# Three stage borders of a two-block transformer kernel: where TensorE claims its banks, and behind which products the turns of the fourth token tile stand

## The chip, the core and the metric

The kernel runs on one core of a Trainium2 chip. A core has TensorE (PE in the profile; PEld is its weight load), VectorE (DVE), ScalarE (ACT), GpSimd (POOL) and SyncE (SP), which run side by side, each through its own list of instructions in order, and wait for one another by semaphores. The metric is the device time of one execution in microseconds (us).

## The reference, cut to what matters

512 tokens of width 1024 go through two blocks. The first mixes attention and pooling by two gates, applies an output product `w_o`, a norm and a residual sum, and then a convolved, gated feed-forward part. The second starts with a norm and a wide product `w_in`, and goes on with two attentions, an output product, a mixture of 32 experts and a last gate.

```python
def first_block(x, ...):
    ...
    mix = (g_a * y_a + g_b * y_b) @ w_o[l]                       # border 1 stands ahead of this product
    x = x + rms_norm(mix, norm_mix_post[l])
    f = conv_gated_ffn(rms_norm(x, norm_ffn_pre[l]), w_up[l], ...)   # border 2: norm, then x @ w_up
    x = x + rms_norm(f, norm_ffn_post[l])
    return x

def second_block(x, ...):
    ...
    a = rms_norm_2(h, g_mix[i])                                  # border 3: norm, then a @ w_in
    proj = a @ w_in[i]
    ...
    h = h + hier_moe(rms_norm_2(h, g_ffn[i]), w_rg[i], w_re[i], w1[i], w3[i], w2[i])
    ...
```

Everything is float32.

## The kernel before, in words

**Tiles.** The tokens are four tiles of 128 (`t` = 0 to 3). X stays in on-chip memory as 128 partitions x 4 tiles x 1024. The eight PSUM banks take the results of TensorE, 128 x 512 each. Which product goes into which bank is fixed by a table (`ps`). `claim(e, key)` waits until the product that stood in that bank before has been read out (semaphore `out_of`, one for each bank), `filled` waits until the bank is written, and `taken` until it has been read.

**Products in three parts.** A dense weight is loaded in units of 128 x 2048. ACT rounds a unit to its high part `w_hi` (L607) and DVE takes the rest as `w_lo` (L612); the activations exist as `HTH` and `HTL` in the same way. A product is then three matmuls for each piece of 128 rows: high by high, high by low, low by high. `split_ready` waits for the low part of a unit (`split_lo_done`). The next unit's split waits until the unit in its buffer has been used; for some units the semaphore `w_used` tells that.

**A norm between two products.** For each token tile DVE scales X by the reciprocal root (L685, semaphore `n_scaled`), TensorE turns the scaled tile with 8 transposes (`norm_pe`, L717: "the turns" of a tile), ACT copies the turned halves to `HTH` (L671) and DVE writes `HTL` (L691). `ht_ready(e, R, t)` waits for that L691. Before the scaling stands the residual sum of the tile: L737 or L745 and L764/L770 (squares and products), L773, L780 (X), L665, L667, L680. The four tiles go through this staggered, in one list on ACT and one on DVE (`stagger`), and the split of a weight unit stands in the middle of it.

**Border 1, the output product (`wo_pe`, about 302 us).** The last products ahead of it are the gates (L788), whose results ACT takes by a sigmoid (L1218) and DVE multiplies (L1267). `wo_pe` claims four banks, one for each token tile, then runs the product of the first half of the rows for four tiles (`j` = 0, 12 matmuls a tile, L1245, from `MIXH` and `MIXL`), and the second half.

**Border 2, the start of the feed-forward part (`ffn_pe`, about 351 to 382 us).** In this order: the turns of tile 1, `uv` for tile 0, the turns of tile 2, `uv` for tile 1, the turns of tile 3, `ug` for tiles 0 and 1 (two outputs `j` of 24 matmuls with 256 columns), then `uv` and `ug` for tiles 2 and 3. All these are L800.

**Border 3, the start of the second block (`qk_pe`, about 720 to 748 us).** Turns of tile 1; the first half of unit pair `in2` for tiles 0 and 1 (L831); turns of tile 2; the second half for tiles 0 and 1 (L819); turns of tile 3; both halves for tiles 2 and 3. After the last first-half product TensorE raises `w_used`, for which ACT's next split (L607) waits, and behind that split stand ACT's squares of the results (L1572), DVE's sums and scalings (L1627, L1638, L1648) and POOL's rotations (L1657, L1659, semaphore `h_qn`). TensorE turns the rotated tiles (L1555) between the products of the next units.

The order on each engine is written out by hand in these functions; no scheduler moves it. The loads of the weights are issued by SP (L878, and L2209 for the experts), each as soon as its place in memory is free.

Of the kernel before, what the change touches and what calls it, by code (L numbers as in the profile page):

```python
# [17 lines left out]
TT, KD = 4, 8  # L18
# [112 lines left out]
def build(nc, x_d, wd, w1_d, w3_d, w2_d, cols_d, rows_d, cst_d, wr_d, wpg_d, pT_d, tb_d, nb_d, out_d):  # L131
    with ExitStack() as ctx:
# [3 lines left out]
        def sem(name):  # L136
            return ctx.enter_context(nc.semaphore(name))
# [83 lines left out]
        w_used, split_hi_done, split_lo_done = sem("w_used"), sem("split_hi_done"), sem("split_lo_done")  # L221
# [247 lines left out]
        def claim(e, key):  # L469

            b, _, emptied = ps.at[key]
            if emptied:
                e.wait_ge(out_of[b], emptied)
            return bank[b], full[b]
# [36 lines left out]
        for n in range(NDENSE):  # L511

            b = n if n < NS else (n - TWO) % 2 if n >= TWO else (2, 3, 1, 0)[(n - A_TWO) % 4] if n >= A_TWO else n % 2
# [108 lines left out]
        def split_ready(e, key):  # L622
            e.wait_ge(split_lo_done, split_index(unit[key]) + 1)
# [84 lines left out]
        def norm_pe(e, R, t):  # L708
            if R != 4:
                e.wait_ge(n_scaled, 4 * R + t + 1)  # L710
            for h in range(2):
                if R == 4:
                    e.wait_ge(n_gained, 2 * t + h + 1)
                b, fills = claim(e, ("n", R, t, h))
                for k in range(4):
                    at = (4 * h + k) * 128
                    m = e.transpose(b[:, k * 128:(k + 1) * 128], norm_xs(R, t)[:, at:at + 128], ident)  # L717
                m.then_inc(fills, 1)

        def ht_ready(e, R, t):  # L720

            for h in range(2):
                taken(e, ("n", R, t, h))
# [67 lines left out]

        ht = [[v[:, k, :] for k in range(KD)] for v in (HTH, HTL)]

        def gemm3_T_part(e, key, outs, ts, last):

            wh, wl = parts(key, KD)
            for j, (b, fills) in enumerate(outs):
                for k in range(KD):
                    for i, (w, src) in enumerate(((wh, HTH), (wh, HTL), (wl, HTH))):
                        m = e.matmul(b[:, ts], w[:, k, j * 128:(j + 1) * 128], src[:, k, ts],  # L800
                                     start=(k == 0 and i == 0), stop=(k == KD - 1 and i == 2))
                if last:
                    m.then_inc(fills, 1)
# [10 lines left out]
        def gemm_tok_part(e, key, j, t, out, low):  # L814

            w = list(parts(key, 4))[low]
            for k in range(4):
                for i, src in enumerate((HTH,) if low else (HTH, HTL)):
                    m = e.matmul(out[:, :], src[:, 4 * j + k, t * 128:(t + 1) * 128], w[:, k, :],  # L819
                                 start=(j == low == k == i == 0), stop=(j == 1 and low == 1 and k == 3))  # L820
            return m

        def high_ready(e, key):
            e.wait_ge(split_hi_done, split_index(unit[key]) + 1)

        def gemm3_tok(e, key, j, t, out):

            wh, wl = parts(key, 4)
            for k in range(4):
                for i, (src, w) in enumerate(((HTH, wh), (HTH, wl), (HTL, wh))):  # L830
                    m = e.matmul(out[:, :], src[:, 4 * j + k, t * 128:(t + 1) * 128], w[:, k, :],  # L831
                                 start=(j == k == i == 0), stop=(j == 1 and k == 3 and i == 2))
            return m
# [405 lines left out]
        def mix_tok(e, key, j, t, out):  # L1239

            wh, wl = parts(key, 4)
            for k in range(4):
                hi, lo = mix_parts(4 * j + k)
                for i, (src, w) in enumerate(((hi, wh), (hi, wl), (lo, wh))):
                    m = e.matmul(out[:, :], src[:, t * 128:(t + 1) * 128], w[:, k, :], start=(j == k == i == 0),  # L1245
                                 stop=(j == 1 and k == 3 and i == 2))
            return m
# [44 lines left out]


        def wo_pe(e):
            bs = [claim(e, ("wo", t, 0)) for t in range(TT)]
            for j in range(2):
                split_ready(e, ("wo", j))
                e.wait_ge(mt_lo, 4 * j + 4)
                for t in range(TT):
                    m = mix_tok(e, ("wo", j), j, t, bs[t][0])  # L1300
                    if j:
                        m.then_inc(bs[t][1], 1)
                if j == 0:
                    m.then_inc(w_used, 1)
            for t in range(TT):
                b, fills = claim(e, ("wo", t, 1))
                for j in range(2):
                    split_ready(e, ("wo", 2 + j))
                    m = mix_tok(e, ("wo", 2 + j), j, t, b)
                m.then_inc(fills, 1)  # L1310
                if t == 2:
                    norm_pe(e, 1, 0)
# [33 lines left out]
        def ffn_pe(e):  # L1346
            outs = {v: [claim(e, (v, j)) for j in range(2)] for v in ("uv", "ug")}
            norm_pe(e, 1, 1)
            split_ready(e, ("uv", 0))
            ht_ready(e, 1, 0)  # L1350
            gemm3_T_part(e, ("uv", 0), outs["uv"], slice(0, 128), False)
            norm_pe(e, 1, 2)
            ht_ready(e, 1, 1)
            gemm3_T_part(e, ("uv", 0), outs["uv"], slice(128, 256), False)
            norm_pe(e, 1, 3)
            split_ready(e, ("ug", 0))
            gemm3_T_part(e, ("ug", 0), outs["ug"], slice(0, 256), False)
            ht_ready(e, 1, 2)
            ht_ready(e, 1, 3)
            gemm3_T_part(e, ("uv", 0), outs["uv"], slice(256, 512), True)  # L1360
            gemm3_T_part(e, ("ug", 0), outs["ug"], slice(256, 512), True)
            for s, (us, ds) in enumerate(FFN):
                for u in us:
                    for j in range(2):
                        for name in ("uv", "ug"):
                            if u:
                                split_ready(e, (name, u))
                                gemm3_T(e, (name, u), 128 * j, *claim(e, (name, 2 * u + j)), *ht)
                for t in range(TT):
                    for h in range(2):  # L1370
                        b, fills = claim(e, ("dn", s, t, h))
                        down_part(e, s, t, h, b).then_inc(fills, 1)
                    if s == LAST and t == 2:
                        norm_pe(e, 2, 0)
# [136 lines left out]
        def qk_pe(e):  # L1511
            bs = [claim(e, ("h", 0, t)) for t in range(TT)]
            norm_pe(e, 2, 1)
            for t0 in (0, 2):
                for j in range(2):
                    if (t0, j) == (0, 1):
                        high_ready(e, ("in2", 1))
                        for t in (0, 1):
                            gemm_tok_part(e, ("in2", 1), 1, t, bs[t][0], 0)
                        split_ready(e, ("in2", 1))  # L1520
                        for t in (0, 1):
                            gemm_tok_part(e, ("in2", 1), 1, t, bs[t][0], 1).then_inc(bs[t][1], 1)
                        norm_pe(e, 2, 3)
                        continue
                    split_ready(e, ("in2", j))
                    for t in (t0, t0 + 1):
                        ht_ready(e, 2, t)
                        m = gemm3_tok(e, ("in2", j), j, t, bs[t][0])
                        if j:
                            m.then_inc(bs[t][1], 1)  # L1530
                        elif t == 3:
                            m.then_inc(w_used, 1)
                    if t0 == 0:
                        norm_pe(e, 2, 2 + j)
            for G in (1, None):
                u = 2 if G else 4
                bs = []
                for j in range(2):
                    split_ready(e, ("in2", u + j))
                    for t in range(TT):  # L1540
                        if j == 0:
                            bs.append(claim(e, ("h", 1, t) if G else ("hv", t)))
                        m = gemm3_tok(e, ("in2", u + j), j, t, bs[t][0])
                        if j:
                            m.then_inc(bs[t][1], 1)
                            qk_turn_pe(e, 4 * (G is None) + t)
                        elif t == 3:
                            m.then_inc(w_used, 1)
# [1655 lines left out]
```

## Time and profile before

| | us |
|---|---|
| median of 3 runs | 1600.0 (1598.81 to 1601.59) |
| the profiled execution | 1599.1 |
| its span, first to last instruction | 1597.2 |
| TensorE busy | 1535.8 (96%) |
| DVE / ACT / POOL busy | 718.2 / 531.1 / 164.6 |
| mean granted clock of TensorE | 0.993 |

The profile is of one execution. A row of the timeline begins with the start and the duration; what stands in brackets at its end is how long the engine was idle before it and who ended that. Matmuls overlap: at full clock one of 512 columns starts about 0.23 us after the one before while its row says 0.39 us, so the distance of starts is what counts.

### The profile page before, as it was taken

The page shows a single profiled execution, that of the slowest core. Times are in us where ns is not written, and L with a number is a line of the kernel's source. Part 1 is how long each engine was busy: PE and PEld are TensorE (multiplying, and loading weights), DVE is VectorE, ACT ScalarE, POOL GpSimd, SP SyncE. Part 2 cuts the span into 40 slices and gives each one's busy share as a digit, 9 for nine tenths or more (in the row PEclk, how much of TensorE's full clock was granted, in tenths as well). Part 3 has the DMA queues.
Part 4 walks back from the last instruction along what each step waited for, and adds up shares of the span by engine and source line. Part 5 has one row for each costly group of instructions (what it writes and reads, how often), then busy time and mean ns, then how long its engine had stood idle before and what let it go on. Part 6 is the DMA issues. An engine that isn't in the chain of part 4 may idle for free.

```text
span 1597.2 us, 19641 instructions
## 1 busy us (share of the span) xinstructions
PE 1535.8 (96%) x7802; PEld 1079.7 (68%) x7802; DVE 718.2 (45%) x1208; ACT 531.1 (33%) x910; POOL 164.6 (10%) x172
## 2 busy tenths in 40 slices
PE   6899999999999999999999999999999999999898
PEld 5666688788888888887777777754444444444367
DVE  5335423455544444468565788432132132132164
ACT  5334422344333423344454577331011011010042
POOL 1013110002211111111300210011000000000000
PEclk9999999999999999999999999999999999999999
DMA  7111322213221323222110231779999999999951
GB/s 271 52 54 60 146 104 105 92 54 119 106 105 57 119 89 106 105 92 81 52 54 27 70 143 56 305 277 387 421 421 421 421 421 420 418 421 421 421 244 54
DMA packets 45437, 311.22 MB, mean 195 GB/s; under 512 B 5136, under 2 KB 5648, under 8 KB 10016
## 3 DMA queue, kind: packets, MB, share of 16 engines
q1 hardware_dynamic: 42336, 296.22, 46.6%
q0 software_dynamic: 3008, 13.72, 2.4%
q8 instruction: 64, 1.05, 0.3%
q14 instruction: 29, 0.24, 0.0%
HBM read 301.52 MB, written 8.39 MB: 194 GB/s over the span
## 4 chain that ended last, share of the span: by engine, by line
PE 87%; DVE 4%; DMA 3%; ACT 3%; issue 2%; DVEq 0%; ACTq 0%; POOLq 0%
PE bank L788 21%; PE bank L2460 13%; PE bank L831 8%; PE bank L1385 6%; PE bank L2476 6%; PE bank L840 6%; PE bank L2443 4%; PE bank L2493 4%; PE bank L1245 3%; PE bank L2659 3%; DMA M<-in_w 3%; PE bank L857 1%; PE bank L800 1%; PE bank L848 1%; PE bank L1986 1%
## 5 line engine op out<-in xcount | busy, mean ns | idle before, releaser
L612 DVE TENSOR_TENSOR w_lo<-M,w_hi 128x2048 fp32r<-128x2048 f32 x73 | 168.8, 2317 | 186.0 <-ACT w_hi L607 186.0
L2460 PE MATMUL bank<-M 128*64 128x512 f32 x1024 | 227.4, 595 | 4.3 <-DMA M<-in_w 4.3
L607 ACT ACTIVATE w_hi<-M 128x2048 fp32r<-128x2048 f32 x73 | 139.0, 1911 | 157.7 <-PE bank L788 56.9
L788 PE MATMUL bank<-HTH,w_hi 128*128 128x512 f32 x432 | 168.1, 389 | 0.0
L788 PE MATMUL bank<-HTL,w_hi 128*128 128x512 f32 x432 | 168.1, 389 | 0.0
L788 PE MATMUL bank<-HTH,w_lo 128*128 128x512 f32 x432 | 168.0, 389 | 0.0
L2460 PEld LDWEIGHTS bank<-M 128*64 128x64 f32 x1024 | 71.5, 137 | 139.8 <-issue 138.6
L2476 PE MATMUL bank<-M 128*64 128x512 f32 x512 | 113.8, 595 | 1.8 <-DMA M<-in_w 1.8
L2618 DVE TENSOR_TENSOR X<-bank,X 128x512 f32<-128x512 f32 x69 | 46.6, 689 | 112.9 <-PE bank L2493 112.8
L788 PEld LDWEIGHTS bank<-HTH,w_lo 128*128 128x128 f32 x432 | 81.1, 188 | 16.9
L788 PEld LDWEIGHTS bank<-HTH,w_hi 128*128 128x128 f32 x432 | 81.1, 188 | 16.8
L788 PEld LDWEIGHTS bank<-HTL,w_hi 128*128 128x128 f32 x432 | 81.1, 188 | 16.7
L2476 PEld LDWEIGHTS bank<-M 128*64 128x64 f32 x512 | 35.9, 137 | 71.6 <-issue 71.5
L2565 ACT ACTIVATE YH<-bank,st 128x512 fp32r<-128x512 f32 x32 | 22.0, 688 | 184.7 <-PE bank L2476 183.3
L831 PE MATMUL bank<-w_hi,HTH 128*128 128x512 f32 x184 | 75.2, 409 | 0.3 <-DVE HTL L691 0.3
L831 PE MATMUL bank<-w_hi,HTL 128*128 128x512 f32 x184 | 72.7, 395 | 0.0
L831 PE MATMUL bank<-w_lo,HTH 128*128 128x512 f32 x184 | 72.4, 393 | 0.0
L2608 DVE SCALAR_TENSOR_TENSOR YL<-bank,st,YH 128x512 fp32r<-128x512 f32 x32 | 24.0, 751 | 104.4 <-ACT YH L2565 103.9
L2595 DVE TENSOR_TENSOR M<-M,bank 128x512 f32<-128x512 f32 x16 | 11.0, 688 | 133.1 <-PE bank L2460 120.4
L1385 PE MATMUL bank<-w_hi,AH 128*128 128x512 f32 x176 | 68.6, 389 | 0.0
L1385 PE MATMUL bank<-w_hi,AL 128*128 128x512 f32 x176 | 68.5, 389 | 0.0
L1385 PE MATMUL bank<-w_lo,AH 128*128 128x512 f32 x176 | 68.5, 389 | 0.0
(365 smaller groups left out, 2875.6 us busy)
## 6 DMA issues: line engine op xcount, KB each, us to landing
M<-in_w SPq DMA_DIRECT2D x192, 1024.0 KB, 10.1
M<-in_wd SPq DMA_DIRECT2D x78, 1024.0 KB, 4.8
M<-in_nb SPq DMA_DIRECT2D x4, 1536.0 KB, 6.5
X<-in_x SPq DMA_DIRECT2D x4, 512.0 KB, 9.2
M<-in_rows POOLq DMA_DIRECT2D x4, 512.0 KB, 6.1
M<-in_tb POOLq DMA_DIRECT2D x8, 256.0 KB, 4.0
rowb<-in_rows POOLq DMA_DIRECT2D x4, 512.0 KB, 5.6
xs_parts<-XSH POOLq DMA_DIRECT2D x1, 2048.0 KB, 10.6
```

The costliest lines, as they stand in the source:

```text
L607: e.activation(hi[:, :], slots[slot_of[n]], ACT.Copy).then_inc(split_hi_done, 1)
L612: e.tensor_tensor(lo[:, :], slots[slot_of[n]], hi[:, :], ALU.subtract).then_inc(split_lo_done, 1)
L788: m = e.matmul(out[:, :], w[:, k0 + k, n0:n0 + 128], v[k], start=(k == 0 and i == 0), stop=(k == len(hi) - 1 and i == 2))
L831: m = e.matmul(out[:, :], src[:, 4 * j + k, t * 128:(t + 1) * 128], w[:, k, :], start=(j == k == i == 0), stop=(j == 1 and k == 3 and i == 2))
L840: m = e.matmul(out[:, :], w[:, k, n0:n0 + 128], src[:, k, :], start=(k == i == 0), stop=(k == 7 and i == 2))
L1245: m = e.matmul(out[:, :], src[:, t * 128:(t + 1) * 128], w[:, k, :], start=(j == k == i == 0), stop=(j == 1 and k == 3 and i == 2))
L1385: m = e.matmul(out[:, :], src[:, a, t * 128:(t + 1) * 128], w[:, i % 2, h * 512:(h + 1) * 512], start=(i == 0 and q == 0), stop=(i == len( ...
L2443: m = e.matmul(b[:, kk * 256:(kk + 1) * 256], v[:, t, k * 128:(k + 1) * 128], S[:, t, :], start=(t == 0 and q == 0), stop=(t == 3 and q == 1))
L2460: m = e.matmul(b[64 * s:64 * s + 64, :], Xe[:, 4 * kh + k, o + C * s:o + C * s + C], unit_w(key, 4)[:, k, :], start=(kh == 0 and k == 0), ...
L2476: m = e.matmul(b[64 * s:64 * s + 64, :], hT[p % 2][:, kk * 128 + 64 * s:kk * 128 + 64 * s + 64], unit_w(key, 2)[:, k, h * 512:(h + 1) * 51 ...
L2493: m = e.matmul(b[:, :], ST[p % 6][:, t * 128:(t + 1) * 128], Y[p % 3][:, h * 512:(h + 1) * 512], start=(p == SCAT[i][0] and q == 0 and not ...
L2659: m = e.matmul(out, x[:, k, t * 128:(t + 1) * 128], w[:, k % 4, cs], start=start and k == ks[0], stop=stop and k == ks[-1])
```

## The change: one wait cut into four, and turns moved behind other products

In `wo_pe` the claim of a tile's bank moves from the head of the function to the head of that tile's product in the first pass. In `ffn_pe` the turns of tile 3 move behind the first of the two `ug` outputs for tiles 0 and 1, and the wait for the `ug` unit moves ahead with it; `gemm3_T_part` gets an argument for which outputs it runs. In `qk_pe` the loop is written out: the first half for tile 2 stands ahead of the turns of tile 3, and then tile 2 is finished before tile 3 begins, where before both had their first half ahead of their second. No instruction is added or taken away on any engine, and ACT, DVE, POOL and SP keep their order.

```diff
-        def gemm3_T_part(e, key, outs, ts, last):
+        def gemm3_T_part(e, key, outs, ts, last, js=range(2)):
...
-            for j, (b, fills) in enumerate(outs):
+            for j in js:
+                b, fills = outs[j]
...
         def wo_pe(e):
-            bs = [claim(e, ("wo", t, 0)) for t in range(TT)]
+            bs = []
             for j in range(2):
                 split_ready(e, ("wo", j))
                 e.wait_ge(mt_lo, 4 * j + 4)
                 for t in range(TT):
+                    if j == 0:
+                        bs.append(claim(e, ("wo", t, 0)))
                     m = mix_tok(e, ("wo", j), j, t, bs[t][0])
...
             gemm3_T_part(e, ("uv", 0), outs["uv"], slice(128, 256), False)
+            split_ready(e, ("ug", 0))
+            gemm3_T_part(e, ("ug", 0), outs["ug"], slice(0, 256), False, [0])
             norm_pe(e, 1, 3)
-            split_ready(e, ("ug", 0))
-            gemm3_T_part(e, ("ug", 0), outs["ug"], slice(0, 256), False)
+            gemm3_T_part(e, ("ug", 0), outs["ug"], slice(0, 256), False, [1])
             ht_ready(e, 1, 2)
             ht_ready(e, 1, 3)
...
         def qk_pe(e):
             bs = [claim(e, ("h", 0, t)) for t in range(TT)]
             norm_pe(e, 2, 1)
-            for t0 in (0, 2):
-                for j in range(2):
...
+            split_ready(e, ("in2", 0))
+            for t in (0, 1):
+                ht_ready(e, 2, t)
+                gemm3_tok(e, ("in2", 0), 0, t, bs[t][0])
+            norm_pe(e, 2, 2)
+            high_ready(e, ("in2", 1))
+            for t in (0, 1):
+                gemm_tok_part(e, ("in2", 1), 1, t, bs[t][0], 0)
+            split_ready(e, ("in2", 1))
+            for t in (0, 1):
+                gemm_tok_part(e, ("in2", 1), 1, t, bs[t][0], 1).then_inc(bs[t][1], 1)
+            ht_ready(e, 2, 2)
+            gemm3_tok(e, ("in2", 0), 0, 2, bs[2][0])
+            norm_pe(e, 2, 3)
+            gemm3_tok(e, ("in2", 1), 1, 2, bs[2][0]).then_inc(bs[2][1], 1)
+            ht_ready(e, 2, 3)
+            gemm3_tok(e, ("in2", 0), 0, 3, bs[3][0]).then_inc(w_used, 1)
+            gemm3_tok(e, ("in2", 1), 1, 3, bs[3][0]).then_inc(bs[3][1], 1)
```

The order of TensorE's instructions at border 1 before, where the last gate product ends and the output product begins (`out_of3` is bank 3 being read out; `mt_lo` the low parts of the mixed rows):

```order
L788 MATMUL bank7<-HTL,w_hi1 128x512
L788 MATMUL bank7<-HTH,w_lo1 128x512
L1245 MATMUL bank0<-w_hi2,MIXH 128x512 [waits out_of3,split_lo_done,out_of2,mt_lo,out_of1,out_of0]
L1245 MATMUL bank0<-w_lo2,MIXH 128x512
L1245 MATMUL bank0<-w_hi2,MIXL 128x512
```

And of the changed kernel, with the first matmul of each token tile:

```order
L788 MATMUL bank7<-HTH,w_lo1 128x512
L1246 MATMUL bank0<-w_hi2,MIXH 128x512 [waits out_of0,mt_lo,split_lo_done]
...
L1246 MATMUL bank1<-w_hi2,MIXH 128x512 [waits out_of1]
...
L1246 MATMUL bank2<-w_hi2,MIXH 128x512 [waits out_of2]
...
L1246 MATMUL bank3<-w_hi2,MIXH 128x512 [waits out_of3]
```

The wait for bank 3 has moved from the first matmul to the 37th, behind three tiles of 12.

TensorE at border 3 before, from the low-part matmuls of tiles 0 and 1 (banks 6 and 7) on; tile 2 is bank 0, tile 3 bank 1, the turns go to banks 4 and 5, `w_hi0` is the first unit of the pair and `w_hi1` the second:

```order
L819 MATMUL bank7<-w_lo1,HTH 128x512 x4
L717 MATMUL bank4<-cst,M 128x128 [waits out_of4,n_scaled]
L717 MATMUL bank4<-cst,M 128x128 x3
L717 MATMUL bank5<-cst,M 128x128 [waits out_of5]
L717 MATMUL bank5<-cst,M 128x128 x3
L831 MATMUL bank0<-w_hi0,HTH 128x512 [waits out_of3,out_of2,split_lo_done]
...
L831 MATMUL bank1<-w_hi0,HTH 128x512 [waits out_of5,out_of4]
...
L831 MATMUL bank0<-w_hi1,HTH 128x512 [waits out_of3,out_of2,split_lo_done]
...
L831 MATMUL bank1<-w_hi1,HTH 128x512 [waits out_of5,out_of4]
```

And in the changed kernel:

```order
L820 MATMUL bank7<-w_lo1,HTH 128x512 x4
L832 MATMUL bank0<-w_hi0,HTH 128x512 [waits out_of3,out_of2]
...
L717 MATMUL bank4<-cst,M 128x128 [waits out_of4,n_scaled]
L717 MATMUL bank4<-cst,M 128x128 x3
L717 MATMUL bank5<-cst,M 128x128 [waits out_of5]
L717 MATMUL bank5<-cst,M 128x128 x3
L832 MATMUL bank0<-w_hi1,HTH 128x512
...
L832 MATMUL bank1<-w_hi0,HTH 128x512 [waits out_of5,out_of4]
...
L832 MATMUL bank1<-w_hi1,HTH 128x512
```

Twelve matmuls now stand between the products of tiles 0 and 1 and the turns of tile 3, and twelve between these turns and the first matmul that needs what they lead to. Border 2 moves in the same way, with 24 matmuls of 256 columns ahead of the turns and 24 behind.

## Rows read from the trace of the kernel before

**Rows 1.** The page's chain that ended last, by engine, as shares of the span.
```profile
PE 87%; DVE 4%; DMA 3%; ACT 3%; issue 2%; DVEq 0%; ACTq 0%; POOLq 0%
```

**Rows 2.** Waits of TensorE: who waited for whom, us in total, times, longest.
```profile
PE bank L2460 <- DMA M<-in_w: 4.3, 5, 1.3
PE bank L2476 <- DMA M<-in_w: 1.8, 3, 1.3
```

**Rows 3.** Timeline of TensorE at border 1: start, duration, instruction.
```profile
301.84 0.39 PE L788 MATMUL bank<-HTH,w_lo 128*128 128x512 f32 x1
304.11 0.47 PE L1245 MATMUL bank<-w_hi,MIXH 128*128 128x512 f32 x1 [1.88 <-DVE M L1267]
...
309.45 0.39 PE L1245 MATMUL bank<-w_lo,MIXH 128*128 128x512 f32 x1
```

**Rows 4.** Timeline of DVE at border 1.
```profile
296.12 2.49 DVE L1275 TENSOR_TENSOR MIXL<-M,MIXH 128x512 fp32r<-128x512 f32 x4
...
303.06 0.69 DVE L1267 TENSOR_TENSOR M<-bank,M 128x512 f32<-128x512 f32 x1 [3.84 <-ACT M L1218]
303.66 3.58 DVE L1278 TENSOR_TENSOR HTL<-M,HTH 128x512 fp32r<-128x512 f32 x4
```

**Rows 5.** Stretches: length, busy us of each engine, granted clock, DMA share, GB/s.
```profile
305.00:308.20 3.20, 3.20 (x10) 2.47 (x9) 2.45 (x4) 2.43 (x2) 1.06 (x2) 0.52 0.00 0
734.00:737.00 3.00, 1.17 (x10) 1.12 (x10) 1.45 (x2) 0.67 (x2) 0.00 (x0) 1.00 0.47 199
751.00:766.00 15.00, 15.00 (x72) 12.40 (x71) 13.69 (x17) 6.38 (x8) 10.69 (x8) 1.00 0.27 89
864.80:868.00 3.20, 3.20 (x9) 2.53 (x8) 1.90 (x5) 1.31 (x4) 0.00 (x0) 0.52 0.01 5
1300.00:1400.00 100.00, 100.00 (x508) 47.39 (x506) 21.83 (x34) 10.11 (x16) 2.33 (x4) 1.00 1.01 420
```

**Rows 6.** The chain that ended last, in time: pieces of 192 products.
```profile
382.32 43.55 PE bank L788 x192
```

**Rows 7.** Timeline of TensorE at border 2.
```profile
362.54 0.28 PE L800 MATMUL bank<-HTH,w_lo 128*128 128x128 f32 x1
363.95 1.09 PE L717 MATMUL bank<-cst,M 128*128 128x128 f32 x8 [1.14 <-DVE M L685]
364.80 0.37 PE L800 MATMUL bank<-HTH,w_hi 128*128 128x256 f32 x1
...
366.92 0.28 PE L800 MATMUL bank<-HTH,w_lo 128*128 128x256 f32 x1
```

**Rows 8.** Timeline of DVE at border 2.
```profile
356.99 2.29 DVE L612 TENSOR_TENSOR w_lo<-M,w_hi 128x2048 fp32r<-128x2048 f32 x1 [0.83 <-ACT w_hi L607]
...
365.28 1.29 DVE L691 TENSOR_TENSOR HTL<-bank,HTH 128x512 fp32r<-128x512 f32 x2 [1.38 <-ACT HTH L671]
```

**Rows 9.** Timeline of TensorE at border 3.
```profile
732.06 1.97 PE L819 MATMUL bank<-w_lo,HTH 128*128 128x512 f32 x8
735.87 1.09 PE L717 MATMUL bank<-cst,M 128*128 128x128 f32 x8 [1.83 <-DVE M L685]
```

**Rows 10.** Timeline of DVE at border 3.
```profile
732.63 1.28 DVE L691 TENSOR_TENSOR HTL<-bank,HTH 128x512 fp32r<-128x512 f32 x2
...
737.19 1.29 DVE L691 TENSOR_TENSOR HTL<-bank,HTH 128x512 fp32r<-128x512 f32 x2 [1.38 <-ACT HTH L671]
```

**Rows 11.** Behind border 3: ACT's split, POOL's rotations, TensorE's turns of tile 3.
```profile
742.47 1.92 ACT L607 ACTIVATE w_hi<-M 128x2048 fp32r<-128x2048 f32 x1 [3.02 <-PE bank L831]
761.48 2.79 POOL L1657 TENSOR_TENSOR M<-M 128x256 f32<-128x256 f32 x1
764.34 0.73 POOL L1659 TENSOR_TENSOR M<-M 128x256 f32<-128x256 f32 x1
770.94 0.60 PE L1555 MATMUL bank<-cst,M 128*128 128x128 f32 x4
```

**Rows 12.** Waits of SP's queue for the expert weights.
```profile
SPq L2209 <- PE bank L2460: 294.8, 63, 34.3
```

More of the change, by code:

```diff
@@ L1513, in qk_pe @@
             norm_pe(e, 2, 1)
-            for t0 in (0, 2):
-                for j in range(2):
[L1516 to L1534, printed above, removed]
+            split_ready(e, ("in2", 0))
[16 more added lines that the diff above has]
+            gemm3_tok(e, ("in2", 1), 1, 3, bs[3][0]).then_inc(bs[3][1], 1)
             for G in (1, None):
```

## The prediction

> **What bounds the kernel now.** I read the chain that ended last first, then TensorE's waits, then the timelines around the three places that the change touches, and last the far end of the program. The chain is TensorE's for 87% of the span [rows 1]: what takes an idle stretch out of TensorE's list, and puts none in, shortens the kernel, unless something behind it runs on a clock of its own. In the timeline each border shows one such stretch. At border 1 the last gate matmul starts at 301.84 and the first of the output product at 304.11, after 1.88 us idle that a read-out by DVE ended [rows 3]. At border 2 the turns of tile 3 start at 363.95, with 1.14 us idle before them until DVE's scaling of that tile was done [rows 7]. At border 3 the same turns start at 735.87 after 1.83 us idle [rows 9]. The idle figures count from the modelled end of a matmul, so I work with starts: 192 products in a row took 43.55 us, 0.227 us each, with a claim of a bank at every 24th [rows 6].
>
> **Border 1.** With no wait the output product would start at 301.84 + 0.23 = 302.07; it started at 304.11: 2.04 us. What was waited for is bank 3 alone: DVE's last L1267 runs from 303.06 to 303.75, and it had been idle for 3.84 us, so all that it did before had ended by 299.2, the low parts of the first four mixed rows among it (296.12 + 2.49 = 298.6) [rows 4]. In the new order bank 3 is asked for at the 37th matmul, 302.07 + 36 x 0.227 = 310.2, 6.5 us after it is free. The second half of the rows starts 48 matmuls in, at 313.0; the low parts that it needs end at 303.66 + 3.58 = 307.2 [rows 4]. So nothing takes the place of the wait, and 2.04 us go. The three claims that now stand between tiles cost nothing, as the claims inside the 192 products don't.
>
> There is a second part. From 304.11 to 309.45 stand 16 starts, 5.34 us where 16 x 0.227 = 3.63 are due, and the stretch from 305.0 to 308.2 shows a granted clock of 0.52, that is the lower level, 1.2 GHz, where stretches of steady work show 1.00 [rows 3, 5]. Before it fell, TensorE had stood still for 2 us; at border 3, after nearly as long a stop, the clock stayed at 1.00 [rows 5, 9]. So the stop makes the fall possible but doesn't always bring it. With the stop gone 5.34 - 3.63 = 1.71 us go too, where an execution had them. I take half, 0.85; the ends are 0 and 1.71.
>
> The Trainium skill (TensorE: Matmul & The Clock Gate, Part 1: The HAM clock gate) says that how many matmuls run slow differs between runs of one kernel. By that the 1.71 us are in some executions of the kernel before and not in others, and the sum would be 5.1 or 6.9 us and seldom between; the trace, which is one execution, cannot tell how often.
>
> **Border 2.** TensorE could have gone on at 362.54 + 0.11 = 362.65, the distance of starts of the 128-column matmuls there; the turns started at 363.95: 1.30 us. Now 24 matmuls with 256 columns come first. 17 of them took from 364.80 to 366.92, 0.125 each with the slower first [rows 7], so 24 take 3.0 us and the turns are reached at 365.6, 1.7 us after the tile is scaled. Their weight, the `ug` unit, is split by 356.99 + 2.29 = 359.3 [rows 8]; their inputs, tiles 0 and 1, are those that the `uv` products have just read. What could be late next is the low part of tile 3. DVE's L691 ended at 365.28 + 1.29 = 366.57, 2.62 us after the turns began [rows 7, 8]; so now it ends 2.6 + 0.1 us behind their start, and TensorE needs it after the turns (363.95 to 364.80, 0.85) and 24 matmuls (3.0), 3.85 us behind it. 1.1 us to spare. 1.30 us go, and all of it moves with border 1, since this chain of DVE and ACT starts from TensorE's own products.
>
> **Border 3.** The eighth low-part matmul ends its turn at 732.06 + 8 x 0.227 = 733.87; the turns started at 735.87: 2.00 us. In the new order tile 2's first half comes first. It needs L691 of tile 2, which ends at 732.63 + 1.28 = 733.91 [rows 9, 10]; with 0.15 us for the signal a new wait of 0.19 us stands there. Then 12 x 0.227 = 2.7 us of matmuls reach the turns at 736.8, 0.9 us after the scaled tile is there (735.87). L691 of tile 3 ended at 738.48, 2.61 us behind the turns [rows 10]; now TensorE wants it 0.84 + 2.7 = 3.6 us behind them: 0.8 us to spare. 2.00 - 0.19 = 1.81 us go.
>
> One thing here gets later. The release of `w_used` comes with tile 3's first half, formerly the 24th matmul behind the turns and now the 36th of a stretch that begins at 734.06 and has the turns in it: 734.06 + 36 x 0.227 + 0.84 = 743.1 plus its drain and two slower starts, 743.4, where ACT's split began at 742.47 [rows 11]. That is 1.0 us later, and queued behind this split are ACT's squares, DVE's sums and POOL's rotations of the first group. TensorE meets this chain again at the turns of rotated tile 3, at 770.94; POOL was done at 765.07 [rows 11]. Of these 5.9 us the change takes 1.0 + 1.8, and 3.1 are left. The unit that this split makes is wanted only after 48 more matmuls, at about 756.7. I price it at nothing.
>
> **The sum.** 2.04 + 0.85 + 1.30 + 1.81 = 6.0 us; without the clock 5.15, with all of it 6.86. Against the profiled execution, 1599.1: 1593.1 (1592.2 to 1594.0). The median of the runs shown is 0.9 above that execution, which may be chance among three; I go half the way and predict **1593.6 us**, 0.4% below the median. A measurement of this kernel can tell a difference from no change above about 0.2%, 3.2 us.
>
> **Does it reach the end?** In the expert stage the DMA moves 420 GB/s with TensorE busy all the time [rows 5], and TensorE waits for weights only for 4.3 + 1.8 us in sum [rows 2]. If that stream ran from a fixed start, time won before it would turn into waits for it. But SP's own queue waited 294.8 us for TensorE to give memory free [rows 12]: the stream starts, and fills, at TensorE's pace, and moves forward with it.
>
> **The rivals.**
> 1. *The gain is given back in the expert stage* (no change). A DMA engine share of 1.01 [rows 5] speaks for it: there the transfers are as full as TensorE. Against it is that the loads wait for TensorE. If it happened, the end would stay at the profiled 1599 to 1600. Chance 0.06.
> 2. *The clock falls elsewhere instead.* Five stretches of 0.52 stand in this trace, one of them at 864.8 [rows 5], inside attention, where TensorE stops often and briefly. Everything behind border 1 moves by 4 to 6 us, so which of these stops brings a fall is drawn again. Each is worth 1.7 us by the 16 starts of [rows 3]. Two more than before, and a gain of 5.15 is 1.75: 1600.0 - 1.75 = 1598.3. Chance 0.08.
> 3. *The later release at border 3 ends slower.* Place: POOL's rotations ahead of 770.94. Two instructions of one form took 0.73 and 2.79 us there [rows 11], and the eight for the first group 10.7 us in sum [rows 5]; if the new timing made all eight like the long one, 22.3. Above 3.1 us of delay TensorE stands: 11.6 - 3.1 = 8.5 us, and 1600.0 - 5.15 + 8.5 = 1603.4. Against it: nothing in the change gives POOL more work, and the mean of the eight, 1.3 us, is far from the long one. Chance 0.03.
> 4. *One of the three borders keeps its stop*, say because tile 3's low part is late and uses up the 0.8 or 1.1 us: the gain is then 3.3 to 4.9 us, 1595.3 to 1597. Chance 0.10.
>
> **How the numbers follow.** The forecast itself, all three stops gone, has 0.73; its own range is 1591.3 to 1596. To hold 8 in 10 I take in rival 4 and a part of rival 2, and a little below for executions in which a fall in attention goes too: 1591.0 to 1597.6. Faster by over 0.2% (below 1596.8) are the forecast and most of rival 4: 0.84. Within 0.2%: rivals 1 and 2 and the rest of rival 4, 0.13. Slower: rival 3, 0.03.
>
> **What the changed profile would show.** TensorE's waits: no row from L1267 to the output product, and no idle ahead of the turns at borders 2 and 3; at border 3 instead about 0.2 us until L691. Border 1: starts at 0.227 us from the first matmul on, granted clock 1.00. Border 2: turns of tile 3 some 3 us behind the `uv` products. The first split of ACT behind border 3 later against TensorE's stretch, and no wait of TensorE at the turns of the rotated tiles. Behind 750, the same distances as before, all 5 to 7 us earlier, to the end. The prediction is wrong if a wait for L691 of over 1 us appears at border 2 or 3, or if TensorE's waits for the expert weights grow by what the borders gave.

## The result and the profile after

| | before | changed |
|---|---|---|
| median, 6 runs each | 1599.4 us (1597.43 to 1601.59) | 1592.46 us (1586.69 to 1593.08) |
| profiled execution / its span | 1599.1 / 1597.2 | 1593.08 / 1591.2 |
| TensorE busy | 1535.8 | 1536.0 |

The ratio is 0.9951, 95% interval 0.9935 to 0.9966: 0.49% faster, and the forecast of 1593.6 lies 1.1 us above the median. On another chip (e5 below), with 12 runs of the changed kernel beside 35 of the one before, the ratio was 0.9966 (0.9952 to 0.9981), 1592.45 against 1598.23 us. TensorE does as much as before; it stands still less.

TensorE's waits in the changed kernel (who waited for whom, us in total, times, longest):

```profile
PE bank L717 <- DVE M L685: 9.9, 2, 9.4
...
PE bank L2461 <- DMA M<-in_w: 2.9, 4, 1.4
PE bank L2477 <- DMA M<-in_w: 2.8, 3, 1.3
...
PE bank L832 <- DVE HTL L691: 0.3, 1, 0.3
```

No row from L1267 to the output product is left. The scaled tile is waited for at the program's start and once more, no longer at borders 2 and 3. The waits for expert weights are 5.7 us in sum where they were 6.1 [rows 2]: nothing was given back there.

Border 1, TensorE's timeline:

```profile
302.46 0.39 PE L788 MATMUL bank<-HTH,w_lo 128*128 128x512 f32 x1
302.69 0.39 PE L1246 MATMUL bank<-w_hi,MIXH 128*128 128x512 f32 x1
...
306.32 0.39 PE L1246 MATMUL bank<-w_lo,MIXH 128*128 128x512 f32 x1
```

From the last gate matmul to the first of the output product 0.23 us, and 3.86 us to its 17th, where [rows 3] have 2.27 and 7.61. Borders 2 and 3:

```profile
362.42 1.03 PE L717 MATMUL bank<-cst,M 128*128 128x128 f32 x8
363.22 0.36 PE L801 MATMUL bank<-HTH,w_hi 128*128 128x256 f32 x1
...
720.26 0.47 PE L832 MATMUL bank<-w_hi,HTH 128*128 128x512 f32 x1 [0.33 <-DVE HTL L691]
...
728.75 0.84 PE L820 MATMUL bank<-w_lo,HTH 128*128 128x512 f32 x3
729.58 0.47 PE L832 MATMUL bank<-w_hi,HTH 128*128 128x512 f32 x1
...
732.42 1.03 PE L717 MATMUL bank<-cst,M 128*128 128x128 f32 x8
733.21 0.48 PE L832 MATMUL bank<-w_hi,HTH 128*128 128x512 f32 x1
```

The turns of tile 3 have no idle in front of them at 362.42 and 732.42, as [rows 7, 9] had. The new wait of border 3 is the distance from the third of the matmuls at 728.75 (its start 729.20) to 729.58, 0.38 instead of 0.23: 0.15 us. It is the step that the prediction put in for the signal: DVE's L691 of tile 2 ends at 729.43, and the product that needs it starts at 729.58. The bracket at 720.26 belongs to tile 1 and was there before. DVE at the two borders:

```profile
363.69 1.29 DVE L691 TENSOR_TENSOR HTL<-bank,HTH 128x512 fp32r<-128x512 f32 x2 [2.94 <-ACT HTH L671]
...
733.69 1.29 DVE L691 TENSOR_TENSOR HTL<-bank,HTH 128x512 fp32r<-128x512 f32 x2 [2.36 <-ACT HTH L671]
```

At both it ends 2.56 us behind the start of the turns, where [rows 8, 10] have 2.62 and 2.61. Behind border 3, ACT's split, POOL's last rotation of the first group and TensorE's turns of that tile:

```profile
738.95 1.92 ACT L607 ACTIVATE w_hi<-M 128x2048 fp32r<-128x2048 f32 x1 [3.00 <-PE bank L832]
...
760.83 0.74 POOL L1660 TENSOR_TENSOR M<-M 128x256 f32<-128x256 f32 x1
...
764.70 0.60 PE L1556 MATMUL bank<-cst,M 128*128 128x128 f32 x4
```

Against the turns of tile 1 at border 3 the split begins 738.95 - 716.11 = 22.84 us behind them; before it was 742.47 - 720.59 = 21.88: the 1.0 us of the prediction. POOL is done 764.70 - 761.57 = 3.1 us ahead of need, where it was 5.9 [rows 11].

Four stretches of the changed kernel (columns as in [rows 5]):

```profile
80.00:83.30 3.30, 3.30 (x9) 2.53 (x9) 0.03 (x1) 0.00 (x0) 0.00 (x0) 0.50 0.25 97
302.50:306.50 4.00, 4.00 (x19) 3.34 (x18) 2.82 (x3) 2.60 (x5) 1.60 (x1) 1.00 0.00 0
729.00:733.00 4.00, 4.00 (x21) 3.06 (x20) 1.88 (x3) 0.71 (x3) 0.00 (x0) 1.00 0.48 203
1300.00:1400.00 100.00, 100.00 (x507) 47.40 (x506) 22.58 (x36) 11.48 (x18) 2.32 (x4) 1.00 1.01 420
```

Behind border 1 the clock stays at 2.4 GHz. Near 80 us, in attention, it is at 1.2 GHz in both executions.

### The profile page after: what moved, and what is told of

The parts are those of the page before. It is cut to its first block, busy times and chain, and to the rows that moved or that the text cites. A ratio compares the mean times of both kernels' runs of the same rounds, so it can differ in the third digit from the quotient of the medians.

```text
span 1591.2 us, 19637 instructions
## 1 busy us (share of the span) xinstructions
PE 1536.0 (97%) x7802; PEld 1080.1 (68%) x7802; DVE 718.0 (45%) x1208; ACT 531.0 (33%) x910; POOL 164.3 (10%) x172
## 4 chain that ended last, share of the span: by engine, by line
PE 89%; DVE 3%; DMA 3%; ACT 2%; issue 2%; DVEq 0%; ACTq 0%; POOLq 0%
PE bank L788 21%; PE bank L2461 13%; PE bank L832 8%; PE bank L1389 6%; PE bank L2477 6%; PE bank L841 6%; PE bank L2494 4%; PE bank L2444 4%; PE bank L2660 3%; PE bank L1246 3%; DMA M<-in_w 3%; PE bank L801 2%; PE bank L858 1%; PE bank L849 1%; PE bank L1987 1%
## 5 line engine op out<-in xcount | busy, mean ns | idle before, releaser
L788 PE MATMUL bank<-HTH,w_hi 128*128 128x512 f32 x432 | 168.1, 389 | 0.0
L788 PE MATMUL bank<-HTL,w_hi 128*128 128x512 f32 x432 | 168.1, 389 | 0.0
L788 PE MATMUL bank<-HTH,w_lo 128*128 128x512 f32 x432 | 168.1, 389 | 0.0
L788 PEld LDWEIGHTS bank<-HTH,w_hi 128*128 128x128 f32 x432 | 81.1, 188 | 16.9
L788 PEld LDWEIGHTS bank<-HTH,w_lo 128*128 128x128 f32 x432 | 81.1, 188 | 16.8
L788 PEld LDWEIGHTS bank<-HTL,w_hi 128*128 128x128 f32 x432 | 81.1, 188 | 16.8
## 6 DMA issues: line engine op xcount, KB each, us to landing
M<-in_nb SPq DMA_DIRECT2D x4, 1536.0 KB, 6.5
```

The source lines that it names most:

```text
L788: m = e.matmul(out[:, :], w[:, k0 + k, n0:n0 + 128], v[k], start=(k == 0 and i == 0), stop=(k == len(hi) - 1 and i == 2))
```

## Marks, for what single runs cannot tell

The time of one kernel varies over 9 us on a chip (before: 1593.15 to 1602.59 in 35 runs), more than any one border is worth. So each execution is read by distances between fixed instructions of TensorE. **A**: last gate matmul to the turns of tile 1 at border 2. **B**: from there to the first product of the next unit (L788). **C**: turns of tile 1 at border 3 to the first turns of a rotated tile (L1555). The kernel before and the changed one were profiled once each for the result, the others stand under The experiments.

| execution | changed borders | A | B | C |
|---|---|---|---|---|
| before | none | 48.42 | 31.90 | 40.73 |
| changed | 1, 2, 3 | 44.66 | 30.56 | 38.97 |
| e5 | 1, 2, 3 | 44.65 | 30.56 | 38.92 |
| e1 | 1 | 44.66 | 33.33 | 40.72 |
| e10 | 1, again | 44.65 | 33.38 | 40.71 |
| e2 | 2 | 48.41 | 30.59 | 40.71 |
| e3 | 3 | 48.43 | 31.90 | 38.97 |
| e4 | 2, 3 | 48.47 | 30.58 | 38.96 |
| e11 | 1, 3 | 44.66 | 31.90 | 38.93 |
| e6 | all, turns of border 3 late | 44.65 | 30.57 | 40.83 |
| e7 | all, turns of border 2 late | 44.66 | 32.48 | 38.95 |
| e8 | all, long stop at border 1 | 52.15 | 30.57 | 38.90 |
| e9 | all, short stop at border 1 | 45.77 | 30.58 | 38.96 |

A is 3.76 us shorter with the change, B 1.34, C 1.76: 6.86 us. The distance from B's end to the first turns of border 3 is 331.87 or 331.88 us in all thirteen. From C's end to the first turns of the last norm it is 780.60 before and 780.69 changed; over all thirteen it lies between 778.6 and 782.2 (e6 and e8), with the kernels with more and fewer changed borders mixed in it. What the borders gave is not taken back there; the profiled execution of the changed kernel shows 6.0 of it in its span, because it was 0.62 us later at border 1 (302.46 against 301.84) and lost 0.2 behind the last norm.

## The experiments

**e1, e2, e3, e4: one border at a time, and two without the first.** Each is the kernel before with the functions of those borders taken from the changed one, for e1:

```diff
-            bs = [claim(e, ("wo", t, 0)) for t in range(TT)]
+            bs = []
...
+                    if j == 0:
+                        bs.append(claim(e, ("wo", t, 0)))
```

> The kernel before with the change at border 1 alone (banks of the output product claimed tile by tile). Theory (each border's stop is worth its own idle, and the sum goes through to the end): from the last gate matmul to the first matmul of the output product 0.23 us instead of 2.27, no slow clock behind it; the turns of tile 1 of the next norm 3.75 us earlier against the last gate matmul; 2.0 to 3.8 us less in time. Rival 1 (the chain of DVE and ACT behind the output product keeps its own time): the turns of tile 3 at border 2 wait longer by what was won, and the gain shrinks below 1 us. Rival 2 (given back in the expert stage): the waits for expert weights grow by 2 us or more and the time stays within 0.5 us.

Measured: A 3.76 us shorter, C as before, but B 33.33 where it was 31.90. The time: 1595.84 against 1597.85 us, ratio 0.9988 (0.9974 to 1.0002), which does not tell it from no change. The waits at the turns of tile 3 of border 2 had not grown (1.14 us, as before), so rival 1 does not explain B. The clock does:

```profile
352.00:356.00 4.00, 4.00 (x38) 4.00 (x38) 3.50 (x6) 1.45 (x3) 0.53 (x1) 1.00 0.51 156
357.00:360.20 3.20, 2.75 (x13) 2.76 (x14) 1.20 (x3) 1.34 (x3) 0.00 (x0) 0.52 0.44 172
361.00:365.00 4.00, 4.00 (x36) 4.00 (x35) 2.29 (x1) 0.85 (x1) 0.00 (x0) 1.00 0.00 0
```

It fell at border 2 during the stop of 1.14 us (1.30 us by starts): the granted clock is 1.00 from 356.2 to 357.1 and 0.50 from 357.2 on, and the turns start at 357.44. 1.4 us of the 3.76 went back there. None of the theories in the expectation had that.

> The kernel before with the change at border 2 alone (turns of tile 3 behind the first ug output). Theory: no idle before the turns, no wait for the low part of tile 3, 1.30 us less from the uv products of tile 1 to the end of the border; time 1.3 us less, hardly above what can be measured. Border 1 still has its stop of 2.04 us, and whether the clock falls behind it is seen once more. Rival: the low part of tile 3 comes late, a wait for L691 of 0.5 us or more, gain under 0.8 us.

Measured: B 1.31 us shorter, no wait for L691; A unchanged, with the clock at 0.50 behind the stop. Ratio 0.9998 (0.9987 to 1.0008): too small to be seen in the time. The rival falls by the mark.

> The kernel before with the change at border 3 alone (tile 2's first half ahead of the turns of tile 3, tile 2 finished before tile 3). Theory: 1.8 us less between the low-part matmuls and the end of the stretch, and the same at every later mark; POOL's rotations about 1 us later than before, TensorE not waiting for them. Rival: TensorE waits at the turns of the rotated tiles, or for L691 of tile 3, and the gain is under 1 us.

Measured: C 1.76 us shorter. The distance from C's end to the last norm, 778.6 us, lies in the scatter given above. POOL is done 3.1 us ahead of TensorE's turns of the last rotated tile, as in the changed kernel, and there is no wait. Ratio 0.9980 (0.9967 to 0.9993), 1593.99 us. The rival falls.

> Borders 2 and 3 changed, border 1 left as before. Theory: 3.1 us less than before by the marks, 2.0 to 3.8 us more than with all three; the sum of the two alone within 0.3 us by the marks. Rival (they share one gain): less than the sum by over 1 us. The stop of border 1 stands here too: one more execution in which it is seen whether the clock falls behind it. If it falls in every one of the four executions with the stop, the clock part is 1.7 us and not half of that.

Measured: 1.32 + 1.77 = 3.09 us by the marks, the sum of the two alone (1.31 + 1.76) within 0.02; ratio 0.9985 (0.9971 to 0.9999), 1595.58 us. The first matmul of the output product in e2, in the timeline, and the stretch behind it, in the view of windows:

```profile
304.09 0.47 PE L1246 MATMUL bank<-w_hi,MIXH 128*128 128x512 f32 x1 [1.88 <-DVE M L1268]
```

```profile
305.10:308.30 3.20, 3.20 (x9) 2.53 (x8) 2.46 (x4) 2.43 (x2) 0.94 (x2) 0.50 0.00 0
```

The same two in e3:

```profile
301.26 0.47 PE L1245 MATMUL bank<-w_hi,MIXH 128*128 128x512 f32 x1 [1.88 <-DVE M L1267]
```

```profile
302.40:305.60 3.20, 3.20 (x10) 2.49 (x9) 2.46 (x4) 2.43 (x2) 0.82 (x2) 0.52 0.00 0
```

And in e4:

```profile
306.89 0.47 PE L1246 MATMUL bank<-w_hi,MIXH 128*128 128x512 f32 x1 [1.91 <-DVE M L1268]
```

```profile
308.20:311.40 3.20, 3.20 (x9) 2.52 (x8) 2.46 (x4) 2.43 (x2) 0.61 (x2) 0.50 0.00 0
```

With the kernel before that is four of four executions in which the clock fell behind this stop, though they reached it at times 6 us apart. In all four it fell when five or six matmuls had started at full clock, and eight distances of about 0.43 us followed where 0.23 are due: 1.6 us. The other 0.1 us of the 1.71 are slower starts at full clock. So the term of border 1 is 1.7 us in these executions, not half of it. Four executions cannot say that the clock always falls here: at a chance of one half each, four in a row come up once in sixteen times.

**e5: the changed kernel again**, no edit.

> The changed kernel once more, on the chip on which the single borders were tried, to have its marks twice. Theory: gate matmul to 17th matmul of the output product 3.85 us, as in the first execution, turns of tile 1 to the up products of border 2 30.6 us, border 3 39.0 us from the turns of tile 1 to the first turns of the rotated tiles; 6 to 7 us less than before. Rival (the first timing was lucky in the clock): 3 to 4 us less, with the same marks.

It ran on another chip than e1 to e4. Measured: the marks within 0.05 us of the first execution, and 1592.45 against 1598.23 us, 5.8 us less. The interval, 0.9952 to 0.9981, is 3.0 to 7.7 us less and so doesn't exclude the rival's 3 to 4 us by itself; the marks do. Four of the granted clocks among these runs say where most of the spread comes from:

| mean granted clock | before: runs, mean us | changed: runs, mean us |
|---|---|---|
| 0.990 | 6, 1601.2 | none |
| 0.993 | 3, 1599.7 | 4, 1593.4 |
| 0.996 | 9, 1597.1 | 1, 1589.2 |
| 0.998 or 0.999 | 6, 1593.9 | 3, 1588.0 |

At one clock the two kernels are 6 to 8 us apart, and each kernel varies by 5 to 7 us with the clock. Over the 35 runs of the kernel before, time and mean granted clock have a correlation of -0.89.

**e6 and e7: the turns still later.** In the changed kernel the turns of tile 3 go behind both products that now stand around them, at border 3

```diff
-            norm_pe(e, 2, 3)
             gemm3_tok(e, ("in2", 1), 1, 2, bs[2][0]).then_inc(bs[2][1], 1)
+            norm_pe(e, 2, 3)
```

> The changed kernel with the turns of tile 3 at border 3 behind both halves of tile 2 (24 matmuls ahead, none behind). Theory (the low part of tile 3 is ready 2.76 us behind the start of its turns, and 12 matmuls behind them cover that): TensorE waits 1.9 us for L691 in front of tile 3's first product, border 3 takes 40.9 us instead of 39.0, and all of the gain of border 3 is lost. Rival (what counts is only that the turns have no wait in front): no loss.

and at border 2 (`norm_pe(e, 1, 3)` behind the second `ug` output).

> The changed kernel with the turns of tile 3 at border 2 behind both ug outputs. Theory: TensorE waits 1.9 us for L691 behind the turns; from the turns of tile 1 to the products of the next unit 32.5 us instead of 30.6, or 34 if the clock falls behind this stop, where before, with its stop of 1.14 us ahead of the turns, it was 31.9. Rival: as in the run for border 3, no loss.

Measured, the first matmul behind the turns, at border 3 in e6 and at border 2 in e7:

```profile
734.75 0.47 PE L832 MATMUL bank<-w_hi,HTH 128*128 128x512 f32 x1 [1.66 <-DVE HTL L691]
```

```profile
364.88 0.36 PE L801 MATMUL bank<-HTH,w_hi 128*128 128x256 f32 x1 [1.66 <-DVE HTL L691]
```

C is 40.83, B 32.48. The stop has moved from in front of the turns to behind them, 1.9 us by starts, as the theory had it: the whole gain of border 3 is gone, and border 2 is 0.6 us worse than before. The rivals fall. The clock stayed at 1.00 in both (from 732 to 740 us in e6, from 362 to 370 in e7). What makes the change work is that products stand on both sides of the turns. In time neither could be told from the changed kernel: 1593.28 and 1592.83 us, ratios 0.9970 (0.9955 to 0.9984) and 0.9969 (0.9953 to 0.9984) to the one before.

**e8 and e9: other stops at border 1.** At the head of the changed `wo_pe` stands one more wait, in e8 `e.wait_ge(mt_lo, 8)`:

> The changed kernel with one more wait at the head of the output product, for the low parts of all eight mixed rows (which its second half needs anyway). Theory (the slow clock is a consequence of the stop, and costs 1.7 us whatever the stop's length): first matmul of the output product 5.5 us behind the last gate matmul, the 17th 10.9 us behind it, as against 3.85 without the stop and 7.6 with the one of before; 7 us more than the changed kernel. Rival (the slow clock costs in proportion to the stop): the 17th over 12 us behind. Rival (the clock falls at this place whatever stands there, by chance of this program's timing): also a slow stretch in the other run that has no stop.

in e9 `taken(e, ("g", 3, 1, 1))`:

> The changed kernel with one more wait at the head of the output product, for ACT's sigmoid of the last gate product: a stop of about 1 us, half of that of before (first matmul of the output product 1.3 us behind the last gate matmul). If the clock falls behind any stop at this place, the 17th matmul comes 6.6 us behind the gate matmul (1.3 + 3.6 + 1.7); if only behind a longer one, 4.9 us behind, as the stop of 1.14 us at border 2 did not bring the clock down in the kernel before.

Measured in e8, the first matmul of the output product and the stretch behind it:

```profile
307.50 0.79 PE L1246 MATMUL bank<-w_hi,MIXH 128*128 128x512 f32 x1 [5.05 <-DVE HTL L1279]
```

```profile
307.50:311.80 4.30, 4.30 (x10) 3.43 (x11) 2.29 (x1) 0.66 (x1) 0.57 (x1) 0.50 0.43 137
```

The first matmul came 5.44 us behind the gate matmul, the 17th 11.32, A is 7.49 us longer than in the changed kernel: 5.21 us of stop and 2.28 of slow clock. The slow part grew from 1.71 to 2.28 while the stop grew from 2.04 to 5.21, so neither theory is exact: it isn't a fixed price, and far from proportional. What it follows is how many matmuls start at the lower level. The granted clock was 0.50 already from 305.3 to 307.4 us, while TensorE stood still, so the product began slow: ten slow distances of starts, where the kernel before had eight. Measured in e9, the same two:

```profile
303.70 0.50 PE L1246 MATMUL bank<-w_hi,MIXH 128*128 128x512 f32 x1 [0.78 <-ACT M L1219]
```

```profile
303.00:310.00 7.00, 6.30 (x28) 5.18 (x29) 5.50 (x6) 4.65 (x6) 2.17 (x2) 1.00 0.06 11
```

The stop is 0.94 us by starts, the clock stayed up, and A is 1.11 us longer; the other 0.17 us are slower first starts at full clock. So the clock fell in five of five executions that stood still for 2.04 us or more at this place, in none of seven without a stop and not in the one with half a stop. At this place it needs the stop; the third theory falls. But the length of a stop doesn't decide alone. By the same measure, starts, the stop at border 3 is 1.95 to 1.99 us in before, e1, e2 and e10, and those of e6 and e7 are 1.9 us, and the clock fell in none of these six; at border 2 it fell in two of five stops of 1.30 us. What else decides was not tested. In time e8 was 1599.57 us, ratio 1.0005 (0.9991 to 1.0020) to the kernel before: this one stop is worth all that the three borders gave.

**e10 and e11: the clock at border 2.** Border 1 alone again, and borders 1 and 3 together, no other edit.

> Border 1 changed alone, a second execution for the clock at border 2. In the first the clock fell behind the stop of 1.14 us at border 2, where with border 1 as before it did not (two executions). If that follows from what TensorE did before the stop, it falls here again: turns of tile 1 to the next unit's products 33.3 us. If it was chance: 31.9 us. Border 1: 3.85 us from the gate matmul to the 17th, as in the first.

> Borders 1 and 3 changed, border 2 as before. The same question as in the run before it, in another program: 33.3 us at border 2 if the removal of the first stop moves the fall of the clock to the second one, 31.9 if not. Borders 1 and 3 by marks: 3.85 and 39.0 us.

Measured, a stretch of e10 and one of e11, each around the turns of tile 3 at border 2:

```profile
363.40:366.60 3.20, 3.20 (x16) 3.20 (x17) 1.32 (x2) 1.85 (x3) 0.00 (x0) 0.51 0.27 100
```

```profile
358.00:368.00 10.00, 8.86 (x77) 8.72 (x77) 7.13 (x8) 4.33 (x6) 0.53 (x1) 1.00 0.45 160
```

It fell in e10 and not in e11. With e1 that is two of three with border 1 changed, and none of two with border 1 as before. Chance is not excluded by so few; that the removal of the first stop is what lets the second one lower the clock was not shown. What is shown is that the clock can fall at a stop of 1.14 us, and that with border 2 changed as well it did not happen in any of five executions (changed, e5, e6, e8, e9).

## Why the prediction was right

**That the three stops go and nothing takes their place.** Right, one by one: B and C shrank by 1.34 and 1.76 us where 1.30 and 1.81 were worked out, within 0.05 us in every execution in which these borders were changed and their turns not moved again. The reserves that carried it were right too: the low part of tile 3 ends 2.56 us behind the turns (2.6 predicted), and e6 and e7 show that without the 12 or 24 matmuls behind the turns TensorE waits 1.9 us, as the same figures say. The new wait of border 3 was 0.15 us where 0.19 was forecast.

**Border 1's idle.** 2.04 us, and the wait for bank 3 at the 37th matmul never seen. Right.

**Border 1's clock: the term that was mis-sized.** The prediction took 0.85 us, half of 1.71, since one execution could not tell how often the clock falls there. It fell in each of the four executions with that stop, so the term is 1.71 and the sum 6.86 instead of 6.0. The reason that the prediction gave for the half, that a stop makes the fall possible but doesn't always bring it, is what the runs show across the three borders (none of six stops of 1.9 to 2.0 us at borders 2 and 3); only at this border was it never seen to fail.

The Trainium skill (TensorE: Matmul & The Clock Gate, Part 1: The HAM clock gate) says, of matmuls at the start of a kernel, that how many run slow differs between runs of one kernel. The prediction carried that over to border 1, where no run shows it: the fall came in four of four, with eight slow distances in each. In the attention stretches the traces agree: from 80.0 to 83.3 us the granted clock is 0.50 in the first execution of the changed kernel and 1.00 in e5, the same program.

**The base.** 1593.6 was counted from a point between the profiled 1599.1 and the median 1600.0. With 0.86 more of clock it would have been 1592.7; measured were 1592.46 and 1592.45. That both come so near is luck in part: against its own runs of the kernel before the change was worth 6.9 us the first time (the interval is 5.4 to 10.4) and 5.8 the second (3.0 to 7.7). The sum rests on the marks, not on these two medians.

**The release of `w_used`.** 1.0 us later, 3.1 us to spare, no wait. Right; rival 3 did not come near.

**The expert stage.** The weights were waited for 5.7 us instead of 6.1 with the DMA at 420 GB/s as before, and the distance from C to the last norm differs by 0.1 us between the first two executions, in a scatter of 3.6 over all thirteen. Rival 1 falls: a gain of 6.9 us given back would have shown as a distance longer by as much. That the stream moves with TensorE is the reading that fits; it was not tested by itself.

**Rival 2**, the clock falling elsewhere. It did not eat the gain of the whole change, but in e1 it is what happened: of 3.76 us at border 1, 1.4 went back at the next border. The rival was placed in attention and came from a neighbour that the change also removes.

## What to carry to other kernels

When an engine turns a tile for a norm, put products that are already possible on both sides of the turns: ahead, to cover the scaling, and behind, to cover what the turned tile still has to go through; count both in durations. Claim a buffer where it is first written, not at the head of a function. And measure such steps by distances between fixed instructions of one trace: a step of 1.3 us repeated within 0.05 us there, while eleven timed runs could not see it.

## What was not expected of the hardware

Stops are given by starts here. Behind a stop of TensorE of 2.04 to 2.07 us the clock fell from 2.4 to 1.2 GHz each time at one place (four of four), at 1.7 us on top, while at a stop of 1.95 to 1.99 us at border 3 it fell in none of four (before, e1, e2, e10), at one of 1.9 us in none of two (e6, e7), and at one of 1.30 us at border 2 in two of five, for 1.4 us. So the length of a stop doesn't say by itself whether the clock falls; what a fall costs is set by the matmuls that start before the clock is back, 0.2 us for each of 512 columns. A kernel's spread on one chip, 9 us in 1598, goes for the most part with the mean granted clock, 0.990 to 0.998. In thirteen executions TensorE reached the last gate matmul of the first block between 299.0 and 305.0 us.
